# Reordered opening, pool sums in two token ranges, interleaved query and gate groups, and a split last scaling in a hybrid pool and retention encoder block

## The reference, cut to what matters

```python
h = rmsnorm(x, norm1_g) * (1 + sc1) + sh1
proj = h @ w_in                        # columns [pool 1024 | q | k | v | g, 1024 each]
# group A: 4 channel groups, windows 2/4/8/16 tokens
pooled = window_mean(u_pool) - u_pool  # then a 256x256 map and a scale per group
# group B: 4 heads of 256, rotary q and k, chunks of 128 tokens, both directions
ret = retention_forward(q, k, v) + retention_backward(q, k, v)
ret_out = silu(g) * rms_per_head(ret)
x = x + g1 * (concat(pool_out, ret_out) @ w_out)
h2 = rmsnorm(x, norm2_g) * (1 + sc2) + sh2
x = x + g2 * ((silu(h2 @ w_gate) * (h2 @ w_up)) @ w_down)
return rmsnorm(x, final_g)
```

## Time and profile before

| | us |
|---|---|
| median of three runs (3034.22 to 3034.26) | 3034.22 |
| the profiled execution, own time | 3038.96 |
| its span on the slowest core (core 7) | 3037.4 |
| spans of the eight cores | 3027.3 to 3037.4 |
| PE busy, core 7 | 2832.2 (93%) |
| DVE busy | 981.9 (32%) |
| ACT busy | 650.3 (21%) |

### The profile page before, as it was taken

How to read it: one execution, slowest core, us unless ns; L and a number is a source line. 1 busy time by engine, 2 the same in 40 slices (tenths; PEclk the granted TensorE clock), 3 DMA queues, 4 the chain that set the end, 5 groups by cost and what they waited for, 6 DMA issues and landing times.

```text
span 3037.4 us, 38737 instructions; the slowest of 8 cores (3027.3 to 3037.4 us)
## 1 busy us (share of the span) xinstructions
PE 2832.2 (93%) x14544; PEld 1387.2 (46%) x14544; DVE 981.9 (32%) x1786; ACT 650.3 (21%) x1246; POOL 152.7 (5%) x275
## 2 busy tenths in 40 slices
PE   4668689999999999999999999999999999999997
PEld 2334446564655444444444444444444444444443
DVE  1353766777746554111111111111101012121212
ACT  2532225353545433100000000000010001000000
POOL 0001100000000000000000000000000000000010
PEclk8889899999999999999999999999999999999998
DMA  9667387746355579756363363353441575959582
GB/s 180 186 113 137 79 137 134 137 92 132 82 118 185 169 233 201 140 99 108 64 111 73 63 115 77 63 107 73 81 90 47 188 264 166 324 173 319 171 261 102
DMA packets 86089, 425.02 MB, mean 140 GB/s; under 512 B 10416, under 2 KB 18736, under 8 KB 47536
## 3 DMA queue, kind: packets, MB, share of 16 engines
q0 software_dynamic: 39248, 244.86, 40.5%
q1 hardware_dynamic: 46656, 177.67, 17.5%
HBM read 501.66 MB, written 96.47 MB: 197 GB/s over the span
## 4 chain that ended last, share of the span: by engine, by line
PE 79%; DVE 9%; DMA 3%; issue 3%; ACT 2%; another core or an unknown queue 2%; DVEq 0%; SPq 0%; ACTq 0%; POOL 0%; POOLq 0%
PE ps L1333 40%; PE ps L1454 19%; PE ps L655 10%; PE ps L1165 3%; PE ps L768 2%; PE ps L1465 1%; DMA arena<-x 1%; DMA arena<-cs 1%; DVE arena L1219 1%; DVE arena L385 1%; DVE arena L687 1%; PE ps L892 1%; DMA arena<-wsc 1%; ACT arena L447 1%
## 5 line engine op out<-in xcount | busy, mean ns | idle before, releaser
L1333 PE MATMUL ps<-arena 128*128 128x512 bf16 x5632 | 1216.1, 379 | 0.9 <-ACT arena L408 0.9
L1333 PEld LDWEIGHTS ps<-arena 128*128 128x128 bf16 x5632 | 550.9, 98 | 664.8 <-issue 1.1
L1454 PE MATMUL ps<-arena 128*128 128x512 bf16 x2640 | 570.0, 379 | 0.0
L655 PE MATMUL ps<-arena 128*128 128x512 bf16 x2048 | 478.9, 390 | 23.9 <-ACT arena L503 16.7
L1339 DVE TENSOR_TENSOR arena<-ps,arena 128x512 bf16<-128x512 f32 x176 | 121.7, 692 | 1046.1 <-PE ps L1333 1022.4
L1454 PEld LDWEIGHTS ps<-arena 128*128 128x128 bf16 x2640 | 258.3, 98 | 311.5
L1337 ACT ACTIVATE arena<-ps 128x512 f32<-128x512 f32 x176 | 105.1, 598 | 1079.7 <-PE ps L1333 1079.6
L655 PEld LDWEIGHTS ps<-arena 128*128 128x128 bf16 x2048 | 200.2, 100 | 257.9 <-issue 52.1
L1165 PE MATMUL ps<-arena 128*128 128x512 bf16 x1024 | 229.1, 380 | 0.6 <-DMA arena<-wsc 0.6
L1408 DVE TENSOR_TENSOR arena<-ps,arena 128x512 f32<-128x512 f32 x64 | 43.9, 687 | 413.8 <-PE ps L1454 399.1
L385 DVE SCALAR_TENSOR_TENSOR arena<-arena 128x1024 bf16<-128x1024 bf16 x128 | 155.9, 1218 | 6.4 <-DMA arena<-w_ada 3.7
(11 more groups left out here) (116 smaller groups left out, 1500.2 us busy)
## 6 DMA issues: line engine op xcount, KB each, us to landing
arena<-wsc POOLq DMA_DIRECT2D x83, 1024.0 KB, 6.8
arena<-x SPq DMA_DIRECT2D x32, 1024.0 KB, 10.1
arena<-w_ada POOLq DMA_DIRECT2D x24, 1024.0 KB, 11.9
arena<-w_ada POOLq DMA_DIRECT2D x48, 512.0 KB, 6.7
arena<-w_gate POOLq DMA_DIRECT2D x22, 1024.0 KB, 16.5
arena<-w_up POOLq DMA_DIRECT2D x22, 1024.0 KB, 16.5
actd<-arena SPq DMA_DIRECT2D x88, 256.0 KB, 3.7
arena<-w_in POOLq DMA_DIRECT2D x20, 1024.0 KB, 14.4
```

The costliest lines, as they stand in the source:

```text
L655: ins = e.matmul(PS[bank][:, :], lhsT=slab[:, kc, fc * 128:(fc + 1) * 128], rhs=hT[:, kc, tt * 512:(tt + 1) * 512], start=(kc == 0), stop= ...
L1333: ins = e.matmul(PS[bank][:, :].rearrange("p (a b) -> p a b", b=128), lhsT=slab[:, kc, jj * 128:(jj + 1) * 128], rhs=h2T[tt][:, :, kc, :], ...
L1454: ins = e.matmul(PS[bo + m][:, :], lhsT=chv[:, a, m * 128:(m + 1) * 128], rhs=slab[:, a, :], start=(j == 0), stop=(j == NFC - 1))
```

## The change

- **Layout.** hT becomes four tiles that lie whole (`hT[t]`), so that the memory of a tile comes free when that tile's last reader is done.
- **Opening.** The three first pool groups stand ahead of the first new norm, a norm's first half is issued one block ahead of its transposes (`norm_ahead`), the fourth pool group of tile 0 comes between the transposes of blocks 4 and 5, and then blocks 5 to 8 are transposed in a row. Of the odd blocks DVE copies both halves out. Of the four small loads that `small_loads` issued, those for the tables go to `table_loads`.
- **Pool sums.** `pool_win` takes a token range. The widest window (two units) is summed over the tokens 0 to 1015 during tile 2 and over the rest later; each unit's buffer is tracked in four parts. Windows are summed over exactly the needed columns.
- **Tables** become a generator with two temporaries, two steps after each of the next pool groups.
- **First modulation.** Four slabs of sh1 are loaded ahead, in four slots, and seven `mod_step`s follow in a row after tile 3. The other four slabs run beside the pool groups. c is loaded beside them, and its Silu stands between the shifts of tiles 1 and 2.
- **Heads.** q and g groups alternate two and two after a lead of four q groups, with 13 consumer steps to the 16 rounds (before: 8 in the q rounds, 5 in the g rounds). Lanes begin twelve rounds later. The slots of the weight ring are in another order. `precast_out` is gone: all eight slabs of w_out are cast on their way in. A fourth `rstg` buffer lies where a row of the first modulation was.
- **Output projection.** Blocks 8 to 11 too are written straight into place.
- **End.** In the last tile the first 1536 columns are multiplied by final_g ahead of the last column block (`ahead_m`), and `finish_split` shares the last scaling between ACT (1024 columns) and DVE (1024), with a store for each half.

```diff
@@ opening @@
-    for t in range(4):
+    scale_tile(0)
+    pool_group(3, 0, 0)
+    pool_group(3, 1, 0)
+    norm_ahead(4)
+    pool_group(2, 0, 0)
+    norm_ahead(5)
+    next(p1[4], None)
+    pool_group(2, 1, 0)
+    for m in (5, 6, 7):
+        norm_ahead(m + 1)
+        next(p1[m], None)
...
+            if t == 2:
+                for _ in range(3):
+                    next(early, None)
             if t == 3 and q_ == 0:
-                win = pool_win(3, 0)
-                drain(win)
+                drain(early)
+                drain(pool_win(3, 0, CUT, 8 + S))
...
-            ada_load()
-            ada_load()
-    tables()
-    cs_load()
-    cs_load()
-    prefetch_in(5)
+    tabs = tables()
+    prefetch_in(4)
+    for _ in range(7):
+        mod_step()
@@ heads @@
-            if (mstate[0] * 2 + mstate[1] - 16) * 108 < (rounds[0] - 1) * 96:
+            if (mstate[0] * 2 + mstate[1] - 16) * 108 < (rounds[0] - 13) * 96:
                 mod_step()
...
-        run_producer(rope_steps(("q", h), qT, B_qR, B_qT), bc, 1.0)
-        prefetch_in(pos + 6)
         ocons = outs(h)
-        run_producer(g_steps(h), chain_gens(bc, ocons), 0.625)
+        run_producer(alternate(rope_steps(("q", h), qT, B_qR, B_qT), g_steps(h), 4, lambda p_=pos: prefetch_in(p_ + 6)), chain_gens(bc, ocons), 0.8125)
@@ w_out @@
-        if i < 8 - NWS:
-            sc.dma("pool", d_, flat, w_out[i], writes=[B_])
-        else:
-            sc.dma("pool", d_, flat, wsc[i - (8 - NWS)], reads=[B_wsc[i - (8 - NWS)]], writes=[B_])
+        sc.dma("pool", d_, flat, w_out[i], writes=[B_])
```

More of the change, by code:

```diff
@@ L603, in tables @@
             lb = lg[:, 4 + h:5 + h]
[L604 to L607, removed]
-            sc.op("act", lambda e, h=h: e.activation(out=DmT[:, h, :], in_=ttmp, func=AF.Exp), reads=[B_rt[0]], writes=[B_T, B_tabm])
@@ L616, in build_nc @@
-    rdT = [B_T, B_tabm]
+            tt_, Bt = tmp()
+            sc.op("dve", lambda e, lf=lf, tt_=tt_: e.tensor_scalar(out=tt_, in0=Am, scalar1=lf, scalar2=LN16, op0=ALU.mult, op1=ALU.add),
+                  reads=[B_cm, B_T], writes=[Bt])
+            sc.op("dve", lambda e, lb=lb, tt_=tt_: e.scalar_tensor_tensor(out=tt_, in0=Bm, scalar=lb, in1=tt_, op0=ALU.mult, op1=ALU.add),
+                  reads=[B_cm, B_T], writes=[Bt])
+            sc.op("act", lambda e, h=h, tt_=tt_: e.activation(out=DmT[:, h, :], in_=tt_, func=AF.Exp), reads=[Bt], writes=[B_tabm])
@@ new lines, in tables @@
+            yield
+            for w_, (row, l_) in enumerate(((rF, lf), (rB, lb))):
+                tt_, Bt = tmp()
+                sc.op("dve", lambda e, row=row, l_=l_, tt_=tt_: e.tensor_scalar(out=tt_, in0=row, scalar1=l_, scalar2=LN16, op0=ALU.mult, op1=ALU.add),
+                      reads=[B_cm, B_T], writes=[Bt])
+                sc.op("act", lambda e, h=h, w_=w_, tt_=tt_: e.activation(out=rowfb[:, h, w_, :], in_=tt_, func=AF.Exp), reads=[Bt], writes=[B_tabm])
+                yield
@@ new lines, in pool_win @@
+        up = upad[u]
+        shs = (1, 2, 4)[:gi]
+        rngs = [(a, b)]
+        for sh in reversed(shs):
+            rngs.insert(0, (rngs[0][0] - sh, rngs[0][1] + sh))
+        l0, h0 = rngs[0]
+        Bu = [B_up[u][t] for t in range(4) if up_cut[t] < h0 and up_cut[t + 1] > l0 - 1]
+        sc.op("dve", lambda e: e.tensor_tensor(out=sa[:, l0:h0], in0=up[:, l0 - 1:h0 - 1], in1=up[:, l0:h0], op=ALU.add),
+              reads=Bu, writes=[B_sa])
+        cur, curB, oth, othB = sa, B_sa, sb, B_sb
@@ new lines, in pool_win @@
+        for sd, c0 in ((0, 8), (1, S)):
+            if not a <= c0 < b:
+                continue
+            sc.op("dve", lambda e, cur=cur, sd=sd, c0=c0: e.tensor_tensor(
+                out=etmp[:, sd * 8:sd * 8 + 8], in0=cur[:, c0:c0 + 8], in1=edge_sb[:, gi, sd, :], op=ALU.mult), reads=[curB, B_edge], writes=[B_etmp])
+            sc.op("dve", lambda e, sd=sd, c0=c0: e.tensor_tensor(
+                out=po[:, c0 - 8:c0], in0=etmp[:, sd * 8:sd * 8 + 8], in1=up[:, c0:c0 + 8], op=ALU.subtract), reads=[B_etmp] + Bu, writes=[Bp])
@@ L1021, in build_nc, with norm_ahead @@
     units_a = [(3, 0), (3, 1), (2, 0), (2, 1)]
-    for t in range(4):
+    def norm_ahead(m):
+        next(p1[m])
+        if m + 4 < NCH:
+            xload(m + 4)
+    scale_tile(0)
[9 more added lines that the diff above has]
+        next(p1[m], None)
+    small_loads()
+    early = chain_gens(pool_win(3, 0, 8, CUT), pool_win(3, 1, 8, CUT))
+    for t in range(1, 4):
         scale_tile(t)
@@ L1082, in build_nc @@
         lane_load()
-    for t in range(4):
+    for t in range(2, 4):
         shift_tile(t)
```

188 lines of the change are left out of this document (109 added, 79 removed).

## The result

The changed kernel takes 2999.92 us (median of 5 runs, 2998.9 to 3018.5), the kernel before 3034.26 beside it: a ratio of 0.989, 95% interval 0.987 to 0.992. That is 34.3 us less, where 60.3 were forecast: the time is 3 us above the range. In some executions of most of these kernels the cores of one die show a lower mean granted clock, down to 0.80; the ratios and the medians of the experiments leave them out, which leaves two executions each of e6_loads and e7_all.

What follows compares the result with a forecast made beforehand. PE was taken as busy at full clock from 450 to 3000 us, with the losses as waits in the first 400. 4.2 + 28 + 19 + 10 - 2 + 1.1 = 60.3 off 3034.22 gives 2974 us, range 2957 to 2997.

Steps and rivals of the forecast that it cites:

- Opening: Start to the end of tile 3 (189.8 us before): tiles follow closer, gain 4.2 us, bounds 0 and 8.
- To k: End of tile 3 to head 0's k (189.8 to 307.54): waits go, gain 28 us, bounds 20 and 31.
- the rule that spoke against this place: First modulation: POOL load descriptors can't be written while DVE holds the port pair; up to 3 us loss, nothing charged.
- k and v of head 0: From 307.54 to 398.25 us: 15.5 us of pool-sum waits and slow clock go; gain 19, bounds 10 and 23.
- Heads: q and g rounds of all heads: fewer state chain waits and no stall; gain 10 us, bounds 3 and 20.
- The alternation: Heads, q alternated with g: state chain waits of some 1.4 us fall from four to three a head.
- The stall: Head 0's q rounds: one 5.8 us wait for a cos/sin load queued beside weight loads and a precast goes.
- The lanes' tail in head 3: Head 3: lanes run until round 120 instead of 109, a loss of 1.4 us.
- w_out: Output projection: last cast slab lands at +91, PE wants it at +89; loss 2 us, bounds 0 and 10.
- End: Last scaling of 2.35 us shared between ACT and DVE: gain 1.1 us, bounds 0 and 2.
- (a): Rival, opening and maps: new waits replace old ones; 2991 us, covering 2983 to 3005; chance 0.20.
- (d): Rival, 83 to 345 us: clock of 0.81 there takes 48 of the 60 us; 3022 us; chance 0.01.

Runs made afterwards that it cites:

- e6_loads: Changed kernel with g's weights issued from the fourteenth k/v round and the next k's after the fifth q/g round: 2991.4 us, 0.984 of before.
- e7_all: Changed kernel with the earlier weight loads, the narrow map's pieces spread over v rounds and four PSUM banks for the state chain: 2970.4 us, 0.977 of before.
- e3_lanes: Changed kernel with the half lanes begun in the first round of head 0's k, as before, instead of the fourteenth: 3008.3 us, 0.990 of before.
- e2_apart: Changed kernel with a head's q groups ahead of its g groups again, state chain steps paced as before: 3000.7 us, 0.987 of before.
- f1_before_banks: Kernel before with the backward state chain's deltas on four PSUM banks in turn: 3026.5 us, 0.996 of before.
- f2_before_nocopy: Kernel before without the bf16 copies of three w_out slabs, all eight cast on loading: 3044.0 us, 1.002 of before.
- e0_again: The changed kernel unaltered, run once more beside its variants: 3002.3 us, 0.988 of before.
- e4_precast: Changed kernel with the bf16 copies of the last three w_out slabs made again behind head 1's weight loads: 3015.8 us, 0.992 of before.
- e5_banks: Changed kernel with the backward state chain's deltas on four PSUM banks in turn instead of two: 2981.9 us, 0.981 of before.
- e1: Changed kernel with the two narrowest units' sums advanced without empty steps, to issue three of the narrow map's pieces in v rounds: 3003.4 us, 0.990 of before.
- e8: Changed kernel with the widest units' sums over the whole range at once, as before: 3003.2 us, 0.988 of before.
- e9: The combination e7_all with q ahead of g again in place of the alternation: 2972.7 us, 0.978 of before.

## Why the prediction was off

**What bounds the kernel.** Right: the time moved in the first 400 us and in the head stages, and nothing between the projection and the end moved at all.

**Opening (forecast 4.2, core 7: 7.2).** 4.3 of the 7.2 came ahead of the first scaled group (83.07 to 78.73 on core 7, 2.6 on the mean of the cores), which the prediction had left out, since "the loads ahead of it are untouched". That part is luck: the first scaled group starts anywhere from 78.6 to 81.0 on the mean of the cores in the changed kernel and its variants, with the same code ahead of it. From there tiles start at 114.1, 139.5 and 166.4: 35.4, 25.4 and 26.8 us apart, where 34.2, 25 and 27.2 were walked. Right in size without the luck: 2.9 of 4.2.

**To k (28; 24.9).** The waits of 16.7 and of 7.2 went, four slabs follow each other with waits of 0.61 and 0.67. The pool wait kept 2.2 where 1.5 was charged. Ahead of k, ACT's shift of tile 0 still leaves 3.95 of the 7.2; that is the missing part. The slabs of sh1 came in time: PE waits for none of them there, so the rule that spoke against this place cost nothing, as charged.

**k and v of head 0 (19; 17.1).** First map without a wait, second with 5.3 (forecast 4.9), its 16 matmuls in 6.5 us (5.6). Right, and by e3_lanes the lanes' delay is 10.5 of it.

**Heads (10; -6.3).** This step failed, by 16 us, and all of the miss on core 7 is in it. Its terms: (1) The alternation. "Three such places a head remain" was to bring 2 us each in heads 1 and 2; the runs say -3.7 in all heads. (The expectation of e2_apart counts head 0's 7.8 to it as well, but most of that is the stall.) The wait is for a PSUM bank, and spreading the steps leaves two deltas in each. The prediction had taken the row for DVE's load in q rounds, where the rotation of two banks was much of it: two more banks bring 11.2 us in the old order (f1_before_banks) and 21.9 in the new one. (2) The stall. "The 5.8 goes with the precasts" held (5.5 in f2_before_nocopy), but the account stopped there: nothing was written down for what POOL's queue held back. The step that moved the lanes counted DVE's time and not the slots that the fourth lane load waits for, nor the two slabs behind it. Freed, head 0 takes 147.1 us on the mean of the cores, 10.7 less, and 7 less than core 7 had. (3) The lanes' tail in head 3 was charged 1.4 and cost 4.9. Against the forecast that makes 7.7, 10.7 and 3.5, together 21.9; from before to e0_again the heads lose 9.7 on the mean of the cores where 10.4 were to be gained, a miss of 20.1. So by stages, on the mean of the cores, the three terms account for the miss within 2 us.

**w_out (-2; 3.4).** Sign wrong, and outside its bounds of a loss of 0 to 10. The slabs land in time (1.3 of wait). On the mean of the cores the stage gains 0.8 in e0_again, so most of the 3.4 is core 7's own.

**End (1.1; 0.2).** The last scaling ends 4.8 us after the last matmul instead of 5.8, but ACT's part is the late one, its half is stored after it, and the span ends as before.

```profile
2975.28 1.15 ACT L1487 ACTIVATE arena<-arena 128x1024 f32<-128x1024 f32 x1 [0.58 <-DVE arena L1486]
```

**From a core to the chip (not in the sum; -12.2).** The forecast took the gain of one core's rows off the median. In it were 4.7 us that the profiled execution had over that median, and the 6.9 us by which another core is now the last.

**The rivals.** (a) named the right kind, new waits in place of old ones, and its 2991 would have been the better number, but its places (slabs in a row, pool sums, tile 1) were all fine; the new wait stood at a fourth one. (d) priced a clock of 0.81 in the front part, from 83 to 345 us. It appeared later, from 356 to 518 us, on two cores, in the profiled one of five executions, and made head 0's stage 172 and 175 us long there instead of 154 to 159, but it does not set the median: no core of the other four executions has a mean clock under 0.98. The Trainium skill (TensorE: Matmul & The Clock Gate, on the peak-current limiter) has the whole die fall once three of its cores run dense matmuls and stay there while the load lasts; here two cores fell while six at the same work did not, and they came back under the same load, so this trace agrees in neither.

## What to carry to other kernels

When work is delayed on one engine, follow the loads whose slots it frees: the queue they stand in holds every load behind them, and lets them go in one burst at the moment the work is finally done. Before a wait on a reader is priced as that engine's load, count the PSUM banks in the rotation; here two more banks were worth 20 us in the new order and 12 in the old, with the same instructions. And a gain read on one core is not the chip's: compare each core with itself, and look which one is last afterwards.

## What was not expected of the hardware

**Cores end in pairs.** In most undisturbed executions one of cores 0 and 1, of 2 and 3, of 4 and 5, of 6 and 7 ended 5 to 12 us ahead of the other (all gaps: 0.3 to 14.5); which one varies. In e4_precast, with the most cast traffic in head 0, the gaps are 8.7 to 14.5 with a median of 12.1; in the two executions of e6_loads, with stores and loads apart, 0.3 to 8.7 with a median of 4.5; in e0_again 2.0 to 11.6 with a median of 7.8. That the traffic makes the gap is not shown, and what the partners share was not measured.

**A granted clock of 0.81 comes to pairs too.** Besides cores 0 and 1 above, the profiled executions of e0_again, e5_banks, e6_loads and e7_all show it for 4 to 5 us near 180 us (e7_all for 3.5 us near 93 too), always on both cores of a pair at once: in e0_again on 6 and 7, not on 5 (windows of cores 6 and 5):

```profile
180.00:187.00 7.00, 7.00 (x37) 3.31 (x35) 1.73 (x4) 1.19 (x2) 0.53 (x1) 0.88 0.38 78
```
```profile
180.00:187.00 7.00, 5.30 (x42) 3.35 (x40) 0.16 (x1) 1.34 (x3) 1.19 (x3) 1.00 0.63 110
```

The profiled executions of the kernel before and of f1 and f2 show only the levels 1.00 and 0.50, but so do those of e1 to e4, e8 and e9, which have the changed opening too. The four that show it near 180 us ran on one chip, these six on two others. So the changed code alone does not bring it; whether the chip does, and what trips it, stays open.
